# Two products of one fp32r weight tile joined into a 512-column matmul, in a transformer block on one core of Trainium2

## What is computed

```python
z  = rms_norm(x, norm_mix) @ w_in                    # then gMLP, dilated and sparse attention
x  = x + concat(out_a, out_b, out_c) @ w_out
x  = x + cross_attention(x, mem) @ xattn_wo
x  = x + square(relu(rms_norm(x, norm_mlp) @ w_up)) @ w_down
...
mods = silu(c) @ w_ada + b_ada                       # 6 columns of 2048
q, k, v, g, a, p, bg = split(modulated(x) @ w_in_2)  # gated linear attention, pooling
y  = merge(gla @ w_gla_out, pool @ w_pool_out, bg) @ w_out_2
x  = layer_norm(alpha * x + mod * y)
x  = layer_norm(alpha * x + mod * (silu(h @ w_g) * (h @ w_u)) @ w_ffn_out)
```

## Time and profile before

| | before |
|---|---|
| median of 3 runs | 3264.18 us (3262.81 to 3266.84) |
| the profiled execution | 3265.56 us, of which the span of instructions is 3264.2 |
| PE busy | 3096.2 us, 95% |
| weight loads busy | 2957.9 us, 91% |
| DVE busy | 2077.1 us, 64% |
| ACT busy | 1416.9 us, 43% |
| DMA | 649.47 MB, 199 GB/s |
| granted TensorE clock, mean | 0.973 of 2.4 GHz |

### The profile page before, as it was taken

One profiled execution on the slowest core, in us unless ns is written; L12 is line 12 of the kernel. 1 busy time (PEld: TensorE's weight loads), 2 busy tenths in 40 slices (PEclk: granted clock), 3 DMA queues, 4 the chain that ended last, 5 costly groups with the idle time before them and its releaser, 6 DMA issues. The chain is left out here.

```text
span 3264.2 us, 53578 instructions
## 1 busy us (share of the span) xinstructions
PE 3096.2 (95%) x23492; PEld 2957.9 (91%) x23492; DVE 2077.1 (64%) x2694; ACT 1416.9 (43%) x1760; POOL 8.5 (0%) x21
## 2 busy tenths in 40 slices
PE   8999998999999999988799998999998999999997
PEld 7988898999999999966788788989997999999997
DVE  5445765899998856675546565556867674444546
ACT  4434544543443434345445454443433444344333
POOL 0000000000000000000000000000000000000000
PEclk9999998999999999988899999999998999999998
DMA  6445343677777855673354544557744775555552
GB/s 245 171 165 178 105 143 117 229 258 275 268 262 283 309 176 192 230 264 139 123 181 150 179 157 154 191 220 269 292 157 163 276 258 181 181 181 182 182 188 81
DMA packets 92745, 649.47 MB, mean 199 GB/s; under 512 B 10304, under 2 KB 10304, under 8 KB 16096
## 3 DMA queue, kind: packets, MB, share of 16 engines
q1 hardware_dynamic: 85968, 621.86, 53.2%
q10 hardware_dynamic: 4608, 16.78, 1.4%
q0 software_dynamic: 1936, 7.41, 0.6%
HBM read 635.51 MB, written 10.49 MB: 198 GB/s over the span
## 5 line engine op out<-in xcount | busy, mean ns | idle before, releaser
L1786 DVE TENSOR_TENSOR RL<-RW,RH 128x1024 fp32r<-128x1024 f32 x974 | 1184.6, 1223 | 830.6 <-ACT RH L1077 828.0
L1077 ACT ACTIVATE RH<-RW 128x1024 fp32r<-128x1024 f32 x974 | 1021.2, 1056 | 1241.5 <-PE b L459 1141.9
L456 PE MATMUL b<-AH,RH 128*128 128x256 f32 x4544 | 1316.0, 290 | 54.0 <-DVE RL L1786 27.1
L458 PE MATMUL b<-AL,RH 128*128 128x256 f32 x4544 | 1299.7, 286 | 0.0
L459 PE MATMUL b<-AH,RL 128*128 128x256 f32 x4544 | 1299.2, 286 | 0.0
L456 PEld LDWEIGHTS b<-AH,RH 128*128 128x128 f32 x4544 | 887.0, 195 | 66.2 <-issue 29.3
L458 PEld LDWEIGHTS b<-AL,RH 128*128 128x128 f32 x4544 | 887.4, 195 | 3.7 <-issue 3.3
L459 PEld LDWEIGHTS b<-AH,RL 128*128 128x128 f32 x4544 | 886.3, 195 | 0.0
L456 PE MATMUL b<-HH,RH 128*128 128x256 f32 x2304 | 652.7, 283 | 2.0 <-DVE RL L1786 2.0
L459 PE MATMUL b<-HH,RL 128*128 128x256 f32 x2304 | 650.6, 282 | 0.0
L458 PE MATMUL b<-HL,RH 128*128 128x256 f32 x2304 | 649.8, 282 | 0.0
(11 more groups left out here) (262 smaller groups left out, 1695.2 us busy)
## 6 DMA issues: line engine op xcount, KB each, us to landing
RW<-in_w_fin SPq DMA_DIRECT2D x88, 1024.0 KB, 4.9
G<-in_w_ada SPq DMA_DIRECT2D x80, 1024.0 KB, 7.1
RW<-in_w_up SPq DMA_DIRECT2D x64, 1024.0 KB, 5.0
RW<-in_w_down SPq DMA_DIRECT2D x64, 1024.0 KB, 5.1
RW<-in_w_fout SPq DMA_DIRECT2D x44, 1024.0 KB, 4.9
RW<-in_w_in SPq DMA_DIRECT2D x40, 1024.0 KB, 5.0
RW<-in_w_v SPq DMA_DIRECT2D x32, 1024.0 KB, 4.9
RW<-in_w_bg SPq DMA_DIRECT2D x32, 1024.0 KB, 4.9
```

The costliest lines, as they stand in the source:

```text
L456: t.matmul(out, wh[:, k, cols], xh, start=first and k == 0 and mm % 2 == 0, stop=False, skip_group_check=True)
L458: t.matmul(out, wh[:, k, cols], xl, start=False, stop=False, skip_group_check=True)
L1077: a.activation(m.high(x), m.slot(j)[:, x % 2 * HC:x % 2 * HC + HC], ACT.Copy).then_inc(s["hi"], 1)
L1786: v.tensor_tensor(m.low(x), m.slot(j)[:, x % 2 * HC:x % 2 * HC + HC], m.high(x).bitcast(F32), ALU.subtract).then_inc(s["lo"], 1)
```

## The change

- In form T the high and the low part of the input become one tensor, and one matmul with the weight's high part moves both, as 512 columns. A second one with the weight's low part moves the high 256 columns. The two give a sum of high products in columns 0 to 255 of a bank and the product with the input's low part in columns 256 to 511.
- A half is now 4 k-tiles x 2 groups of 128 columns, a block 256 weight columns (4 halves where K is 2048), still with a pair of banks.
- After each block ACT copies the low sums to SBUF (`LT`), and DVE adds them: in `summed`, `summed_in_place`, `add_both` or `gated`.
- Low parts of the weights are written over the chunk in RW. There are 5 slots and a ring of 5 high parts; a slot is refilled when PE has used both halves.
- The first two blocks of some products are interleaved (`zipped`), and the input's k-tiles are prepared in other groups (`FED`).
- The column 4 of `ada` moves from the MLP to the stretch from `gout` to `out2`, beside column 3, and the pauses change.

```diff
-NW, NR = 4, 4
+NW, NR = 5, 5
...
+FED = ((0, 1), (2,), (3,), (4,), (5, 6), (7,))
+def steps(blocks, halves, zipped=False):
+    out = [(b, c) for b in range(blocks) for c in range(halves)]
+    if zipped:
+        out[:2 * halves] = [(0, 0), (1, 0), (0, 1), (1, 1), (0, 2), (0, 3), (1, 2), (1, 3)]
+    return out
...
     def low(self, n):
-        return self.RL[:, n % NR * HC:n % NR * HC + HC]
+        at = SPLIT[n // 2] % NW * CH + n % 2 * HC
+        return self.RL[:, at:at + HC]
...
-                    for mm in range(4):
-                        out = bb[mm // 2][:, (mm % 2) * 256:(mm % 2) * 256 + 256]
-                        cols = slice(mm * 128, mm * 128 + 128)
-                        for k in range(2):
-                            xh, xl = hi(2 * c + k), lo(2 * c + k)
-                            t.matmul(out, wh[:, k, cols], xh, start=first and k == 0 and mm % 2 == 0, stop=False,
-                                     skip_group_check=True)
-                            t.matmul(out, wh[:, k, cols], xl, start=False, stop=False, skip_group_check=True)
-                            done = t.matmul(out, wl[:, k, cols], xh, start=False, stop=last and k == 1,
-                                            skip_group_check=True)
+            for k in range(4):
+                if b == 0 and k % 2 == 0:
+                    need(2 * c + k // 2)
+                x = x2(4 * c + k)
+                for mm in range(2):
+                    bank = m.banks[2 * ((g0 + b) % 2) + mm]
+                    cols = slice(mm * 128, mm * 128 + 128)
+                    t.matmul(bank[:, :], wh[:, k, cols], x, start=first and k == 0, stop=False, skip_group_check=True)
+                    done = t.matmul(bank[:, 0:256], wl[:, k, cols], x[:, 0, :], start=False, stop=last and k == 3,
+                                    skip_group_check=True)
...
+    def low_part(g):
+        a.wait_ge(s["used"], num.half)
+        a.activation(pair2(m.LT[g % 2]), m.sum_l[g % 2], ACT.Copy).then_inc(s["lt"], 1)
...
+    def summed(out, g):
+        v.wait_ge(s["lt"], num.lt)
+        v.tensor_tensor(pair2(out), m.sum_h[g % 2], pair2(m.LT[g % 2]), ALU.add).then_inc(m.pair[g % 2], 1)
+        v.wait_ge(m.pair[g % 2], g // 2 + 1)
...
+            for i in range(2):
+                x = m.X[:, (2 * p + i) * S:(2 * p + i + 1) * S]
+                part = m.LT[g % 2][:, i * S:i * S + S] if low else m.sum_h[g % 2][:, i, :]
+                r = v.scalar_tensor_tensor(x, part, m.mod(which, 2 * p + i), x, ALU.mult, ALU.add)
...
-                y.wait_ge(s["lo"], HALF_OF[was] + 2)
+                y.wait_ge(s["used"], HALF_OF[was] + 2)
...
-    beside = chain(L.ada((0, 1, 4), (2.4, 2.4, 1.6)), L.ctx_loads())
+    beside = chain(L.ada((0, 1), (3.4, 3.4)), L.ctx_loads())
...
-    beside = when(L, L.ada((3,), (2.0,)))
+    beside = when(L, L.ada((3, 4), (1.4, 1.4)))
```

More of the change, by code:

```diff
@@ L428, in wait_empty, with block_begins, gemm, gemm_n @@
             t.wait_ge(bk.empty, bk.n - 1)
-    def gemm(blocks, kc, hi, lo, form, need, beside=None):
-        rest = None
+    def block_begins(g):
+        if g >= 2:
+            t.wait_ge(m.pair[g % 2], g // 2)
+    def gemm(blocks, halves, x2, need, zipped=False, beside=None):
+        rest, g0 = None, num.block
+        num.block += blocks
+        for b, c in steps(blocks, halves, zipped):
+            n = num.half
+            num.half += 1
+            if c == 0:
+                block_begins(g0 + b)
+            t.wait_ge(s["lo"], n + 1)
+            wh = m.high(n).rearrange("p (k n) -> p k n", k=4)
+            wl = m.low(n).rearrange("p (k n) -> p k n", k=4)
+            first, last = c == 0, c == halves - 1
+            for k in range(4):
[8 more added lines that the diff above has]
+                                    skip_group_check=True)
+            done.then_inc(s["used"], 1)
+            if rest is not None:
+                next(rest, None)
+            yield
+            if last:
+                if num.factor is not None:
+                    next(num.factor, None)
+                if beside is not None:
+                    rest = beside(b)
+                    next(rest, None)
+                if b % 2 == 1 and b + 1 < blocks:
+                    yield
+        yield
+    def gemm_n(blocks, hi, lo, need):
         for b in range(blocks):
@@ L1485, in v2, with evac, k2, q2 @@
         num.v += 1
-        yield from gemm(1, 4, copied(dst))
+        def evac(b, g):
+            a.wait_ge(s["used"], num.half)
+            for i in range(2):
+                r = a.activation(dst[:, i * 512:i * 512 + 512], m.banks[2 * (g % 2) + i][:, :], ACT.Copy)
+            r.then_inc(m.pair[g % 2], 1)
+            yield
+        yield from gemm_n(1, evac)
+    def k2(use):
+        yield from gemm(4, 4, nothing)
+    def q2():
+        yield from gemm(4, 4, nothing, True)
     L.low_rank, L.k2, L.q2, L.v2 = low_rank, k2, q2, v2
@@ L1787, in prepare, with gemm, gemm_n @@
                             ALU.subtract).then_inc(s["lo"], 1)
-    def gemm(blocks, kc, evac):
+    def gemm(blocks, halves, evac, zipped=False):
+        rest, g0 = None, num.block
+        num.block += blocks
+        for b, c in steps(blocks, halves, zipped):
+            prepare(num.half)
+            num.half += 1
+            if rest is not None:
+                next(rest, None)
+            yield
+            if c == halves - 1:
+                num.lt += 1
+                if rest is not None:
+                    exhaust(rest)
+                if num.factor is not None:
+                    next(num.factor, None)
+                rest = evac(b, g0 + b)
+                next(rest, None)
+                if b % 2 == 1 and b + 1 < blocks:
+                    yield
+        exhaust(rest)
+        yield
+    def gemm_n(blocks, evac):
         rest = None
```

940 lines of the change are left out of this document (464 added, 476 removed).

## The result

| | before | after |
|---|---|---|
| median | 3263.49 us (4 runs, 3259.15 to 3266.84) | 3222.88 us (4 runs, 3221.22 to 3225.97) |
| ratio to before | | 0.9877, 95% interval 0.986 to 0.9895 |
| span of the profiled execution | 3264.2 us | 3224.7 us |
| granted clock, mean | 0.973 | 0.968 |

The changed kernel is 41 us faster; 3225 was forecast. The page's line of engines answers to the earlier trace rows. PE has 6896 instructions fewer and is busy 66 us less, DVE is busy 158 us more.

What follows compares the result with a forecast made beforehand. PE's full queue was taken as the bound, with DVE as slow in `pout`. Terms -90 + 27 + 8 + 3 + 11 + 2 = -39 us took 3265.6 to 3226.6, forecast as 3225 us against 3264.2; range 3192 to 3275.

Steps and rivals of the forecast that it cites:

- The tile, 347 ns, and a half of 2.78 us: PE, form T: a weight tile goes from 360 to 347 ns, a half from 2.88 to 2.78 us.
- The rival without a gain: PE, form T: a tile keeps its 360 ns, fewer weight loads save nothing; 3307 us, chance 0.07.
- the figure of the Trainium skill named above: PE: full-clock matmul gap of N / 2.4 + 2.5 ns, a tile from 328 to 325 ns, 17 us of gain.
- -90 us: PE, all 6896 weight tiles: two matmuls in place of three save 13 ns each.
- +27, +8, +3: `pout` and `out2`: DVE's added work +27 us, late tiles of `ada` +8, column 4's reductions at the end of `out2` +3.
- +11, +2: Eight places where PE waits for results, 1.4 us each, +11 us; starts of `w_in` and the MLP +2.
- The sum of 51 against 50: Whole kernel: all cost terms beside PE's gain together, 51 us forecast.
- DVE late in `pout` and `out2`: `pout` and `out2`: DVE needs 159 us of work against PE's 131; PE's waits for low parts grow to about 60 us.
- The +8 for late tiles of `ada`: `out2`: DVE waits for 12 tiles of `ada`, 0.7 us each, +8 us; bounds 0 and 21.
- Zeros: No cost in MLP and feed-forward, `gout`, the start of `fin`, the slot refill after `used`, or block starts.
- the cover of 1.1 us a block: MLP and feed-forward: DVE needs 10.0 us a block against PE's 11.1, so its added work costs 0.
- My rival: `pout` and `out2`: the clock falls, a third of 48 halves at 1.2 GHz; 3248 us, chance 0.06.

Runs made afterwards that it cites:

- the repeat: The changed kernel as it is, measured once more for the spread between profiled executions: 3228.84 us, ratio 0.9886.
- the balanced one: The changed kernel with column 4 of `ada` back beside the MLP, pauses 2.8, 2.8, 1.5 and 2.5: 3208.51 us; with three matmuls a tile 3259.14 us.
- e1_three: The changed kernel with the 512-column matmul split again, so three matmuls of 256 columns a weight tile: 3276.39 us, ratio 1.0041.
- e4_half_acc: The changed kernel with DVE's accumulations for columns 3 and 4 of `ada` taking only 256 of each 512 columns: 3205.88 us (one run).
- e5_fetch_once: The changed kernel with only the first two tiles of columns 3 and 4 of `ada` fetched and used for all: 3228.32 us, ratio 0.9894.
- e8_four_slots: The changed kernel with 4 slots for the weights in place of 5: 3229.56 us, ratio 0.99.

## Why the prediction was right, and where it was not

- **The tile, 347 ns, and a half of 2.78 us**: right. The 13 ns belong to the instruction. The rival without a gain and the figure of the Trainium skill named above are both out.
- **"-90 us" as a term of the sum**: mis-sized in place. It multiplied all 6896 tiles by 13 ns, and so took every stage for PE's. Measured: 54 us in the changed kernel (48 against the repeat), 51 in the balanced one. Of the 36 missing only 4 are in `pout` and `out2`; the rest is spread over `bg2`, the first `fin`, the first `up`, parts of `down` and short stages, which I had treated as PE's.
- **"+27, +8, +3"**: right as to what they are, 7 too much in sum. I had added them on top of PE's new share, and measured in that way they are 31 us for 38. Without the merged matmul the same stretch is 27 us longer than before.
- **"+11, +2"**: 13 for everything else, where 19 was measured over PE's new share, and not at the places that I named. 8 of it are the heads of `bg2`, put at nothing, and 4 the first `fin`; the first two stages came out 4 shorter.
- **The sum of 51 against 50** is therefore in part luck: 7 too much at one place, 6 too little at the others. It also isn't the cost of the rest of the change, as my expectation for `e1_three` took it (3308; measured 3276). It is what the stages take over a PE share that many of them don't follow. The two readings differ by the same 36 to 38 us, once as a missing gain and once as a missing cost.
- **DVE late in `pout` and `out2`**: right in place and near in size. `e4_half_acc` shows that DVE's load sets it, `e5_fetch_once` that the transfers don't. A block of `pout` took 58.2 / 8 = 7.3 us, the number of my count. The route to PE was not the one named: bank pairs, the sum of x and transposes, not low parts of weights.
- **The +8 for late tiles of `ada`**: nearly absent. DVE waited 2.1 us there; with half the accumulation it waited 8.9, so the tiles come next once DVE has less to do. The new slack for weights made theirs the transfers that land late.
- **Zeros**: the refill after `used` holds (`e8_four_slots`). The MLP's holds at the pause of 3.4, with 88.8 us for 32 halves; the cover of 1.1 us a block is real but thin, as the sum done twice and column 4 show. There I had left out that DVE also waits for ACT's copies, which wait for DVE.
- **A slip**: I counted 214 T blocks, all halves by four; `outa`, `outb`, `pout`, `xo` and the last `fout` have shorter blocks, and the low copies are 234. That is 20 x 0.7 = 14 us more of DVE's work; what it costs in time was not tried.
- **The clock**: 0.92 in `pout` with `out2`, less than before (0.98). My rival priced this at 23 us on top; the stretch came out under the forecast instead. The lower clock is a part of the 31 us all the same: the waits that end in the stretch or just behind it are 29 us against 11 before, and the rest, some 12, is about what 0.92 for 184 us and 0.98 for 158 make (an estimate from these rows). While DVE is the later engine a slower PE costs nothing more; how much it costs at the end of `out2`, where the two take turns, no run tells.

## What to carry to other kernels

Cost a change stage by stage, as the largest of the engines' new loads, and give a PE gain only to those stages where PE's matmuls follow each other without a gap; a gain per tile times all tiles was 35 us too much here. Where a change has a gain and a cost, say for each term whether it is measured against the kernel before or against the other term. Where work can lie beside several stages, spread it: column 4 of `ada` back beside the MLP at a slower pace made the kernel 14 us faster than the change as made, and the same column at the old pace made it 14 us slower. A wait on an engine that runs ahead tells nothing yet: 105 us of new waits of ACT for transfers cost no time that could be measured.

## What the runs showed of the hardware

- fp32r matmuls on different weight tiles with 512 and 256 moving columns in turn start 347 ns a pair apart, 27 ns more than the columns at 2.4 GHz, and 350 where the input is tile H, for which I have no cause; with three matmuls both took 360.
- A transfer of 1 MB landed in 4.8 us on the median of most weights over the span, and from 2200 to 2290 us, where weights and tiles of `ada` together moved 331 GB/s, in 6.7 to 7.2 for the weights and 5.0 for `ada`.
- In the first `v2`, with the same instructions, the granted clock was 0.90 to 0.93 from kernel to kernel and the stage 151.6 to 158.3 us. The longest three (157.5 to 158.3) had 0.90 and the shortest (151.6) 0.93, but 0.91 went with 152.0; which caused which, no run here tells.
